# A two-network transformer kernel on one core: first products of the next stage drawn into the tails of the attentions, and the third mixer's output projection by head pairs

## The reference, cut to what matters

```python
def layer(x, cx, ..., need_ctx):
    ...
    px = split_cols(hx @ w_in)
    pc = split_cols(hc @ w_in)
    ya, yca = global_gqa(...)
    yb, ycb = neighbourhood_attn(...)
    yc_, ycc = window_gqa(...)
    ux = jnp.concatenate([ya, yb, yc_], axis=-1) * jax.nn.silu(px[9])
    x = x + gate[:, None, :] * (ux @ w_out)
    if need_ctx:
        uc = jnp.concatenate([yca, ycb, ycc], axis=-1) * jax.nn.silu(pc[9])
        cx = cx + gate_c * (uc @ w_out)
    return x, cx
```

## Time and profile before

| | |
|---|---|
| profiled execution, its own time | 1963.6 us |
| its span from first to last instruction | 1961.7 us |
| TensorE matmul busy | 1882.5 us, 96% |
| VectorE busy | 1279.5 us, 65% |
| ScalarE busy | 1098.7 us, 56% |
| GpSimd busy | 96.9 us, 5% |
| mean granted TensorE clock | 0.993 |
| DMA | 287.42 MB, 146 GB/s |

### The profile page before, as it was taken

How to read it: one execution, slowest core, us unless ns; L and a number is a source line. 1 busy time by engine, 2 the same in 40 slices (tenths; PEclk the granted TensorE clock), 3 DMA queues, 4 the chain that set the end, 5 groups by cost and what they waited for, 6 DMA issues and landing times.

```text
span 1961.7 us, 33814 instructions
## 1 busy us (share of the span) xinstructions
PE 1882.5 (96%) x13140; PEld 1630.6 (83%) x13140; DVE 1279.5 (65%) x2075; ACT 1098.7 (56%) x1915; POOL 96.9 (5%) x86
## 2 busy tenths in 40 slices
PE   6999999999899898999999999999999999999997
PEld 4977877877778787888988898889888889898886
DVE  5652354456843666876668588777776677587766
ACT  4372255274553647775456467764775555567753
POOL 2000000001200001400100010001000100010001
PEclk9999999999999999999999999999999999999999
DMA  8231242232313231455543245555555542255453
GB/s 315 87 130 65 87 150 108 86 123 72 108 67 127 80 125 66 171 192 193 211 157 109 87 172 193 192 175 190 193 181 189 215 156 100 93 189 191 175 191 148
DMA packets 42504, 287.42 MB, mean 147 GB/s; under 512 B 4928, under 2 KB 6336, under 8 KB 8848
## 3 DMA queue, kind: packets, MB, share of 16 engines
q1 hardware_dynamic: 40832, 280.33, 39.7%
q0 software_dynamic: 1552, 5.39, 0.9%
HBM read 284.65 MB, written 1.05 MB: 146 GB/s over the span
## 4 chain that ended last, share of the span: by engine, by line
issue 49%; PE 37%; DVE 6%; ACT 4%; POOL 3%; DMA 1%; SPq 0%; DVEq 0%; POOLq 0%; ACTq 0%
PE bank L2042 7%; PE bank L2044 7%; PE bank L2043 7%; PE bank L2048 6%; PE bank L2049 3%; PE bank L2219 2%; PE bank L2238 2%; PE bank L2196 2%; DVE panels_lo L1376 1%; ACT work L1011 1%; POOL work L808 1%; PE bank L2115 1%; PE bank L2230 1%; PE bank L2177 1%; POOL xT L849 1%
## 5 line engine op out<-in xcount | busy, mean ns | idle before, releaser
L1376 DVE TENSOR_TENSOR panels_lo<-raw_panels,panels_hi 128x1024 fp32r<-128x1024 f32 x472 | 581.9, 1250 | 228.8 <-ACT panels_hi L880 226.9
L2048 PE MATMUL bank<-acts,panels_hi 128*128 128x512 f32 x2032 | 717.0, 398 | 3.7 <-DVE xT L1794 1.7
L880 ACT ACTIVATE panels_hi<-raw_panels 128x1024 fp32r<-128x1024 f32 x472 | 488.5, 1054 | 298.2 <-PE bank L2044 191.4
L2049 PE MATMUL bank<-acts,panels_lo 128*128 128x256 f32 x2032 | 570.1, 281 | 0.0
L2048 PEld LDWEIGHTS bank<-acts,panels_hi 128*128 128x128 f32 x2032 | 381.4, 188 | 97.1 <-DVE xT L1794 1.9
L2049 PEld LDWEIGHTS bank<-acts,panels_lo 128*128 128x128 f32 x2032 | 383.9, 189 | 0.2
L2042 PE MATMUL bank<-acts,panels_hi 128*128 128x256 f32 (+1 forms) x984 | 302.3, 307 | 5.2 <-DVE xT L1794 1.4
L2043 PE MATMUL bank<-acts,panels_hi 128*128 128x256 f32 (+1 forms) x984 | 298.3, 303 | 0.0
L2044 PE MATMUL bank<-acts,panels_lo 128*128 128x256 f32 (+1 forms) x984 | 298.3, 303 | 0.0
L2042 PE MATMUL bank<-panels_hi,acts 128*128 128x512 f32 (+1 forms) x640 | 227.4, 355 | 8.8 <-DVE acts L1496 3.5
L2044 PE MATMUL bank<-panels_hi,acts 128*128 128x512 f32 (+1 forms) x640 | 223.6, 349 | 0.0
(11 more groups left out here) (253 smaller groups left out, 1970.9 us busy)
## 6 DMA issues: line engine op xcount, KB each, us to landing
raw_panels<-weights SPq DMA_DIRECT2D x256, 1024.0 KB, 4.8
token_major<-weights SPq DMA_DIRECT2D x4, 1024.0 KB, 12.0
near_bias<-rpb POOLq DMA_DIRECT2D x16, 256.0 KB, 3.1
xT<-xin SPq DMA_DIRECT2D x4, 512.0 KB, 5.8
gates<-weights SPq DMA_DIRECT2D x2, 1024.0 KB, 11.9
near_bias<-weights SPq DMA_DIRECT2D x2, 512.0 KB, 6.4
out<-xT SPq DMA_DIRECT2D x4, 256.0 KB, 2.2
work<-weights SPq DMA_DIRECT2D x2, 256.0 KB, 6.6
```

The costliest lines, as they stand in the source:

```text
L880: act.activation(slot_hi(n, a, b), raw_of(n, a, b), ACT.Copy).then_inc(hi_ready, 1)
L1376: dve.tensor_tensor(slot_lo(n, a, b), raw_of(n, a, b), slot_hi(n, a, b).bitcast(F32), ALU.subtract).then_inc(lo_ready, 1)
L2048: pe.matmul(bank.rearrange("p (c t) -> p c t", c=2), whi_, with_rest(xhi_), start=start, stop=False, skip_group_check=True)
L2049: return pe.matmul(bank[:, 0:T], wlo_, xhi_, start=False, stop=stop, skip_group_check=True)
```

## The change

1. **Ahead products.** `attention` takes a function `ahead`. In the iterations after the last scores of attention A and B it issues the first quarter of the next `qkv` for its first two tiles (in layer 0's B both in the last but one iteration), in attention C a part of `wout("C")`, in the second block the last branch gate, each before the last value products rather than after them.
2. **`token_half`** waits for the banks of tiles 0 and 1 at its start and for those of tiles 2 and 3 only when it comes to them.
3. **`wout("C")`, first panel**, goes by head pairs: for kt = 0..3, both steps. Both steps end at kt = 3.
4. **Layer 0's attention C** does its four context steps first, then the eight of latents.
5. **VectorE in the attentions** takes the maxima of step i before it inverts the sums of step i-1.
6. **The norm of layer 1**: GpSimd adds more of the squares and their two halves, so `token_sums` has 10 matmuls for the latents and 6 for the context; they stand at other places of the last `wout` step; the residual of the last latents goes ahead of the context's of the step before; the first `over_rows_of_tokens` moves into the last `wout` step; one `warming` matmul goes; VectorE's scaling of the context's last tiles and a ScalarE panel half are moved back.

The diff, cut to its core (the four context steps are the new local function `context`; `token_quarter` is the old body of `token_half` for one tile; in 3, `wout_tile` is called for kt = 0..3 at the start of `wout("C")`, less what `wout_ahead` has done):

```diff
+            if with_ctx and mixer == "C":
+                context()
...
-        for squares, ready, added in ((squares_a, sqa_ready, acca_ready), (squares_b, sqb_ready, accb_ready)):
-            pool.wait_ge(ready, 2)
-            pool.tensor_tensor(squares(0), squares(0), squares(1), ALU.add).then_inc(added, 1)
+        add_a(1, 1)
+        halves_a()
+        add_b(1, 1)
+        add_b(1, 2)
+        pool.tensor_tensor(squares_b(0)[:, 0:T], squares_b(0)[:, 0:T], squares_b(0)[:, T:2 * T], ALU.add).then_inc(accb_ready, 1)
...
-                            act.wait_ge(lat_done, q + 1)
-                            act.activation(tile4(squares_a(q), 2), x_pair(q), ACT.Square).then_inc(sqa_ready, 1)
                             if q == 3:
                                 break
+                            for x in range(q, q + 1 + q // 2):
+                                act.wait_ge(lat_done, x + 1)
+                                act.activation(tile4(squares_a(x), 2), x_pair(x), ACT.Square).then_inc(sqa_ready, 1)
...
             scaled_c(2, 0, 3)
-            scaled_c(2, 1, st.at["steps"] + 3)
+            scaled_c(3, 0, 4)
             inverse(cstat[:, 0:4], 2).then_inc(inv_cols, 1)
-            scaled_c(3, 0, 4)
...
             normed(0)
             normed(1)
+            latents_lo(0)
+            normed(2)
+            latents_lo(1)
             begin(st.at["steps"] + 3)
             residual_c(3, 1).then_inc(freed, 1)
-            normed(2)
-            latents_lo(0)
+            latents_lo(2)
             normed(4)
-            latents_lo(1)
+            latents_lo(3)
             normed(6)
-            latents_lo(2)
+            latents_lo(4)
+            scaled_c(2, 1, st.at["steps"] + 3)
             scaled_c(3, 1, st.at["steps"] + 4)
-            latents_lo(3)
-            latents_lo(4)
             inverse(cstat[:, 4:8], 3).then_inc(inv_cols, 1)
...
-                if 0 <= j < len(steps) and steps[j].deferred:
-                    g, un = g0 + j, steps[j].units[0]
-                    ns = len(un.segs)
-                    dve.wait_ge(exped, now(exped, 2 * g + 2))
-                    if un.segs[0][2] is not None:
-                        dve.tensor_tensor(stat2(g, 2, ns), stat2(g, 2, ns), stat2(g, 6, ns), ALU.add).then_inc(dve_chain, 1)
...
+                    g, un = g0 + j, steps[j].units[0]
+                    ns = len(un.segs)
+                    dve.wait_ge(exped, now(exped, 2 * g + 2))
+                    if un.segs[0][2] is not None:
+                        dve.tensor_tensor(stat2(g, 2, ns), stat2(g, 2, ns), stat2(g, 6, ns), ALU.add).then_inc(dve_chain, 1)
+                        dve.wait_ge(dve_chain, chain.next())
...
-                            dve.wait_ge(last_latents, 1)
-                            dve.wait_ge(freed, s)
-                            residual_c(3, 0).then_inc(lat_done, 1)
                             return
                         begin(s)
                         residual_c(q, 0).then_inc(lat_done, 1)
+                        if q == 2:
+                            dve.wait_ge(last_latents, 1)
+                            residual_c(3, 0).then_inc(lat_done, 1)
                         residual_c(q, 1).then_inc(freed, 1)
                         if q < 2:
...
+        def token_half(n, half, banks_of, blk, s, done=()):
...
+                    if half + quarter == 0 and tt in done:
+                        continue
+                    if half + quarter + tt % 2 == 0:
+                        take(s + tt // 2)
+                    o = token_quarter(n, half, quarter, bank, tt, blk)
...
-                for e in range(2):
+                for e in range(2 if q else 1):
...
+                if blk == 2 and i == len(steps) + 2:
+                    ahead(2)
...
+                    if i == slot and i < len(steps) + 2:
+                        branch_gate(st, r)
+                if blk == 1 and i >= len(steps):
+                    ahead(i - len(steps))
...
-                warming(1)
-                over_rows_of_tokens(banks[7], 0)
...
-                        for i in range(tiles // 2):
-                            s += 1
-                            take(s)
-                        token_half(n, 0, pair, 1)
-                        token_half(n + 1, 1, pair, 1)
+                        token_half(n, 0, pair, 1, s + 1, done=(0, 1) if j == 0 else ())
+                        token_half(n + 1, 1, pair, 1, s + 1)
+                        s += tiles // 2
...
-                                token_sums(banks[4], squares_b, (accb_ready, sqb_ready), (0, 2, 3), sumb_done)
+                                token_sums(banks[4], squares_b, (accb_ready, sqb_ready), (0, 3), sumb_done)
...
+            def qkv_ahead(m, k):
...
+                st = ONE["qkv" + m, l]
+                s = st.at["steps"]
+                tiles = {0: (0,), 1: (1,)}.get(k, ()) if m == "B" or not wctx else {1: (0, 1)}.get(k, ())
+                for tt in tiles:
+                    if tt == 0:
+                        take(s)
+                    token_quarter(st.at["panels"], 0, 0, step_banks(s)[tt], tt, 1)
...
+            def wout_tile(kt, halves, done=()):
+
+                st, at = ONE["woutC", l], ONE["attnC", l]
+                for c in halves:
+                    if c in done:
+                        continue
+                    if kt == 0:
+                        take(st.at["steps"] + c)
+                    pe.wait_ge(usplit, at.at["pairs"] + (NPAIR if wctx else 0) + kt + 1)
+                    for e in range(2):
+                        o = wout_product("C", 0, c, e, kt)
+                    if kt == 3:
+                        o.then_inc(tick, 1)
+
+            def wout_ahead(k):
+                if k == 0 and not wctx:
+                    wout_tile(0, (0,))
+                if k == 1 and not wctx:
+                    wout_tile(1, (0,))
+                    wout_tile(0, (1,))
+                    wout_tile(1, (1,))
+                if k == 1 and wctx:
+                    wout_tile(0, (0, 1))
+
...
                 if m != "C":
                     pe.wait_ge(usplit, at.at["pairs"] + at.pairs)
+                if m == "C":
+                    for kt in range(4):
+                        wout_tile(kt, range(2), () if kt > 1 or kt and wctx else range(2))
...
-                                        if part + e == 2 and kt in (0, 2):
-                                            token_sums(banks[6], squares_a, (acca_ready, sqa_ready), *(((0, 2),) if kt == 0 else ((3,), suma_done)))
+                                        if (part, e, kt) == (0, 1, 0):
+                                            token_sums(banks[6], squares_a, (acca_ready, sqa_ready), (0,))
+                                        if (part, e, kt) == (1, 0, 1):
+                                            token_sums(banks[6], squares_a, (acca_ready, sqa_ready), (2,))
+                                        if (part, e, kt) == (1, 0, 3):
+                                            token_sums(banks[6], squares_a, (acca_ready, sqa_ready), (3,), suma_done)
+                                        if (part, e, kt) == (1, 1, 2):
+                                            over_rows_of_tokens(banks[7], 0)
...
+            attention(2, None, False, at, lambda k: branch_gate(at, len(GATE_SLOTS) - 1))
...
```

More of the change, by code:

```diff
@@ L254 @@
 DVE_START2, DVE_LAYER = 182, 73
-POOL_ENTRY = 4
+POOL_ENTRY = 7
 PANELS = START2["panels"] + LAYERS * PER_LAYER["panels"]
@@ L561, in attention_plan, with context @@
             gqa = mixer != "B"
+            def context():
+                for p in range(NPAIR):
+                    idx = p // 2 if gqa else p
+                    units, adds = [], []
+                    for e in range(2):
+                        h = 2 * p + e
+                        keys = k_split(idx, e, 512, T, 2 * T)
+                        units.append(Unit([(q_split(p, e, T + qt * P), keys, qt * T, T) for qt in range(TT)],
+                                          [(qt * T, T, h if mixer == "C" else None, None) for qt in range(TT)], [],
+                                          [(qt * T + b * P, b * T + qt * P) for qt in range(TT) for b in range(2)]))
+                    for b in range(2):
+                        for e in range(2):
+                            vcol = (p // 2 if gqa else 2 * p + e) * HD
+                            adds.append((e, val(2 + b, vcol), e * 512 + b * T, T, 0, b == 0))
+                    steps.append(Step(units, [(0, 512)], adds, len(pairs), True, True, [(qt, qt * P) for qt in range(TT)]))
+                    pairs.append((p, 1))
+            if with_ctx and mixer == "C":
+                context()
             for p in range(NPAIR):
@@ L1540, in attention @@
                 j = i - 1
-                if 0 <= j < len(steps) and steps[j].deferred:
-                    g, un = g0 + j, steps[j].units[0]
-                    ns = len(un.segs)
-                    dve.wait_ge(exped, now(exped, 2 * g + 2))
```

(21 more changed lines are left out.)

74 lines of the change are left out of this document (31 added, 43 removed).

## The result

The kernel after takes 1940.92 us (median of 5 runs, 1939.36 to 1944.08); run beside it, the kernel before had a median of 1956.72 us of 5. The ratio is 0.9905, 95% interval 0.9882 to 0.9927: faster, by 7 to 12 parts in a thousand. A later set of six runs of the same kernel gave 1947.66 us and 0.9932 (0.9913 to 0.9951), so two sets differ by 6.7 us. The profiled execution took 1941.76 us (span 1939.9), 21.8 less than the one before. Forecast: 1947 us, a saving of 16.1.

What follows compares the result with a forecast made beforehand. TensorE, busy 96% of the span, was taken as the bound, with VectorE setting the time up to 526 us. Terms summed to 16.1 us off 1963.6, so 1947.5; with the median 0.5 below, 1947 us, range 1940 to 1957.

Steps and rivals of the forecast that it cites:

- the base: Whole kernel: start from the profiled execution of 1963.6 us, with the median of the runs 0.5 below it.
- the lower clock's term: Layer 1's first panel, 486 to 492.2 us: fewer small instructions in a row bring full clock, -3.1 us; 0 if it stays.
- Tails of A and B in layer 0: Ahead products cover the last values' wait for the gating, 1.14 us in each of two attentions: -2.3 us.
- Banks tile by tile: Second panel pairs, four places in layers 0 and 1: the 0.73 + 0.15 us wait for the last tile's copy goes, -3.5.
- Context first: Layer 0's attention C: tail waits of 3.65 us shrink to 0.52 + 0.15, start loses 0.8; together -2.2 us.
- Projection and norm: Layer 0's C projection by pairs and norm: losses +0.5, +0.4; sums -0.5, -1.5; warming -0.4; first product's wait -1.0; total -2.5 us.
- GpSimd's +1.8: Layer 0's projection and norm: three more GpSimd additions slow VectorE's scalings, one and a half collisions less slack, +1.8 us.
- Maxima before inverses, -3.3, and the last turn's -0.8: Layer 1's attentions: fourth scores' waits end, B -1.7, C -1.3, A -0.3; B's last turn's wait covered by ahead products, -0.8.
- Projection by pairs in layer 1: Tail of layer 1's C and output projection: the first step ends later, a loss of about +0.8 us.
- Second block: Both passes: last branch gate beside the last values' 1.15 + 0.15 us wait, part lost again; -0.5 each, -1.0 us.
- low clock elsewhere: Rival, chance 0.11: the 0.50 clock stretch stays and one of the same length comes at new thin places, 1953 us.
- The slower rival: Rival, chance 0.05: maxima first delays value products in 68 steps; at 0.4 us a step, 1974 us.

Runs made afterwards that it cites:

- Before again: The kernel before once more, with no edit: 1957.89 us, ratio 0.9997 (0.9984 to 1.0009), profiled execution 1955.87 us.

## Why the prediction was right and where it failed

The saving was near: 16.1 forecast, 14.7 in the stages, 15.8 between the medians of the first comparison. Two steps failed most.

The first is the base: "the median of the runs is 0.5 below that execution". The five runs of the first comparison had a median of 1956.72 us, 6.9 below the profiled 1963.6, and 1956.72 - 16.1 is 1940.6 for a measured 1940.92. But that agreement is partly luck. All 28 runs of before from the comparisons (these five and 23 later ones) have a median of 1959.9 us, 3.7 below the profiled execution, and all 11 of after one of 1942.9; 1959.9 - 16.1 is 1943.8. So about half of the 6 us is the base and the rest the spread of small sets. I had three runs, two of which lay near the profiled one, and said that they spread over 9 us; two of the 23 later runs were as long as 1963.6.

The second is the lower clock's term, -3.1. Without it the forecast is 13.0; the stages give 12.8 at equal numbers of low stretches. That these two agree is luck in part as well, since terms in the sum were too small and too large. Term by term:

- **Tails of A and B in layer 0, -2.3:** 2.2 by the experiment.
- **Banks tile by tile, -3.5:** 4.1, slightly under-sized; the idle time was as read, 0.73 in each place, so about 0.3 us stood behind each wait and not 0.15.
- **Context first, -2.2 with the tail of C:** wrong. The first wait grew by 1.14 us (1.20 to 2.34) for 0.8 forecast, and the context last is 0.7 faster. All that the change does in this stage but the norm gives 0.3 (132.13 and 131.86, one low stretch each): the tail had less to gain, because the ahead products cover most of it in either order. What the projection by pairs costs in layer 0 wasn't tried alone.
- **Projection and norm, -2.5, with GpSimd's +1.8:** the norm alone gained 2.7. The waits came out near the forecast (0.39 idle + 0.15 at the third step for 0.5, 0.79 at the first product for 0.6). The +1.8 was read from four scalings that took 3.22 us beside an addition; here such a group stood beside one and took 1.13, while the addition took 2.23. The Trainium skill (SBUF — State Buffer, Who interferes with whom) lets whoever issues first block the other for a whole instruction. The 1.13 and the 2.23 agree with that, VectorE being first; where additions meet panel splits, both engines are stretched (2.27 for 1.44, 3.30 for 2.35). In both kernels VectorE's first scaling started 0.04 to 0.06 us ahead of the addition (460.27 and 460.31, 464.81 and 464.87); why the addition waited for all four here and cut in before is open.
- **Lower clock, -3.1:** wrong in its cause and its size. The old sums in the changed kernel bring no low stretch at 480. Before again, the same code as before, has none there either:

```profile
483.00:489.00 6.00, 4.83 (x37) 4.36 (x37) 3.51 (x5) 4.22 (x10) 3.20 (x4) 1.00 0.00 0
```

  Without it this stage took 1.7 us less and not 3.1 (133.81 to 132.13). At equal numbers the stage became 3.0 us shorter (132.13 to 129.14); forecast without the clock 2.9. The kernel before with maxima first had a shorter one there again (486 to 490), and none of the 11 profiles of the changed kernel and its variants has any; whether something else of the change makes it rarer is open. The prediction also saw only this one; in the same trace two more stand at 526 and 536.
- **Maxima before inverses, -3.3, and the last turn's -0.8:** under-sized. The part alone gives 5.1, with B 2.9 (1.7 forecast), C 2.2 (1.3) and A nothing (0.3). The terms counted the fourth scores' wait; the values' waits for the gating (1.45 in B, 1.01 in C) and a turn's (0.74) went as well. The last turn's wait fell from 0.64 to 0.39 by this part alone, and is 0.17 in the changed kernel without ahead products, so most of it isn't theirs.
- **Projection by pairs in layer 1, +0.8:** 0.9.
- **Second block, -1.0:** 0.8 in the traces, 0.9 in the experiment.

The rival "low clock elsewhere" isn't decided. Stretches stand at 637 and 757 us in the execution after; but before again has one at the start of B too (642). The one at 757 was in 6 of the 9 profiles in which the next stage waits 2.6 us there, and in none of the 5 in which it waits 1.69. The slower rival didn't occur: no stage got longer by maxima first.

## What to carry to other kernels

Take the baseline of a forecast from many runs, and compare two profiles stage by stage: in this kernel stages repeat to 0.1 us, and what differs otherwise comes in a few sizes that can be counted out. Do so with a second profile of the kernel before, ahead of giving a price to anything seen in the first: 3.1 us were forecast here for a stretch that the next execution didn't have. A wait before an instruction is worth filling only if nothing else will cover it; of the fillings here those in layer 1 cost a little. Ask of each engine's order what it does while it waits: taking work that is ready before work that must be waited for gave a third of the whole gain with a move of nine lines.

## What the chip showed that I had not expected

- At a granted clock of 1.00 and with no idle time, TensorE goes through the last loop of products at one of two paces: a pair of matmuls, one of 512 columns and one of 256, started every 353 ns or every 348 ns (30.4 us for 86, 30.6 for 88), the same through the whole loop and another in the next execution. 1.5% of the last products' 211 us is 3.2 us. In the 14 profiles the second and the fourth of the four long loops took either value, the first one of three (up to 4.6 us apart) and the third always the same, so this is a large part of the 9 us between runs. What sets it stays open: instructions, operands and their order are the same in all of them.
- The stretches at the 1.2 GHz level move between executions and with any edit. One cost between nothing beside waits (B of layer 1 in the kernel before: 82.16 us without, 82.13 with one) and 1.6 us where TensorE is busy. They followed thin work (the starts of attentions, the first products after a norm). The Trainium skill (TensorE: Matmul & The Clock Gate, HAM oscillation) names waits between bursts as the cause; the traces agree on the places, but in the same place of the same code it came in some executions only.
